# Decode rows of the output projection as fp32 products in four column groups of the array

## What is computed

```python
m = jax.nn.sigmoid(ga) * (o_a @ w_pa) + jax.nn.sigmoid(gb) * (o_b @ w_pb)
x = x + _rmsnorm(m @ w_o, g_mq)
h = _rmsnorm(x, g_fp)
f = (jax.nn.silu(h @ w_g) * (h @ w_u)) @ w_d
x = x + _rmsnorm(f, g_fq)
```

## Time and profile before

| | us |
|---|---|
| median of 3 runs (1453.14 to 1455.04) | 1453.59 |
| the profiled execution, its own time | 1453.83 |
| its span, first to last instruction | 1452.1 |
| PE busy | 1434.0 (99%) |
| PE weight loads busy | 1387.8 |
| DVE busy | 875.2 |
| ACT busy | 627.8 |
| POOL busy | 322.2 |

### The profile page before, as it was taken

How to read it: one execution, slowest core, us unless ns; L and a number is a source line. 1 busy time by engine, 2 the same in 40 slices (tenths; PEclk the granted TensorE clock), 3 DMA queues, 4 the chain that set the end, 5 groups by cost and what they waited for, 6 DMA issues and landing times.

```text
span 1452.1 us, 26576 instructions
## 1 busy us (share of the span) xinstructions
PE 1434.0 (99%) x10633; PEld 1387.8 (96%) x10633; DVE 875.2 (60%) x1539; ACT 627.8 (43%) x1259; POOL 322.2 (22%) x288
## 2 busy tenths in 40 slices
PE   7999999999999999999999999999999999999998
PEld 6999999999999999997789999999999999999997
DVE  7735766313424438483678966777775667667565
ACT  7335555335524532244676433333333335443561
POOL 2022222000000016060002354655362220010111
PEclk9999999999999999999999999999999999999999
DMA  7112323613212126215564334555543349223632
GB/s 233 30 50 77 97 79 112 184 57 108 73 30 77 30 87 205 61 54 176 196 200 140 99 120 153 193 179 204 167 146 118 95 148 377 82 81 108 228 141 102
DMA packets 168381, 184.90 MB, mean 127 GB/s; under 512 B 17514, under 2 KB 128370, under 8 KB 166852
## 3 DMA queue, kind: packets, MB, share of 16 engines
q1 hardware_dynamic: 164368, 171.09, 36.6%
q0 software_dynamic: 2720, 7.89, 1.8%
q10 hardware_dynamic: 1172, 4.23, 0.7%
HBM read 140.73 MB, written 42.45 MB: 126 GB/s over the span
## 4 chain that ended last, share of the span: by engine, by line
PE 93%; DVE 4%; DMA 1%; ACT 1%; issue 1%; DVEq 0%; ACTq 0%
PE bank L1057 7%; PE bank L1059 6%; PE bank L1058 6%; PE psAB L1601 3%; PE bank L1601 3%; PE psAB L1603 3%; PE psAB L1602 3%; PE bank L1602 3%; PE bank L1603 3%; PE psT L1053 3%; PE bankC L1603 2%; PE bankC L1601 2%; PE bankC L1602 2%; PE bank L1158 2%; PE bank L1160 2%; PE bank L1159 2%
## 5 line engine op out<-in xcount | busy, mean ns | idle before, releaser
L1057 PE MATMUL bank<-h_hi,w_hi 128*128 128x344 f32 x464 | 155.8, 336 | 3.0 <-DVE h_lo L2472 3.0
L1059 PE MATMUL bank<-h_hi,w_lo 128*128 128x344 f32 x464 | 149.3, 322 | 0.0
L1058 PE MATMUL bank<-h_lo,w_hi 128*128 128x344 f32 x464 | 149.2, 322 | 0.0
L2229 ACT ACTIVATE s_hi<-raw 128x512 fp32r<-128x512 f32 x126 | 78.7, 627 | 106.7 <-PE psAB L1603 91.3
L1601 PE MATMUL psAB<-f,s_hi 128*128 128x258 f32 x400 | 113.5, 284 | 0.1
L1603 PE MATMUL psAB<-f,s_lo 128*128 128x258 f32 x400 | 112.7, 282 | 0.0
L2459 DVE TENSOR_TENSOR w_lo<-w_raw,w_hi 128x1024 fp32r<-128x1024 f32 x53 | 65.5, 1235 | 61.3 <-ACT w_hi L1764 61.3
L3027 DVE TENSOR_TENSOR s_lo<-raw,s_hi 128x512 fp32r<-128x512 f32 x126 | 94.7, 778 | 2.7 <-ACT s_hi L2229 2.6
L1057 PEld LDWEIGHTS bank<-h_hi,w_hi 128*128 128x128 f32 x464 | 88.3, 190 | 7.3 <-POOL w_lo L3329 3.2
L1601 PE MATMUL bank<-f,s_hi 128*128 128x258 f32 x328 | 93.0, 283 | 0.6 <-DVE ev L3207 0.4
L1603 PE MATMUL bank<-f,s_lo 128*128 128x258 f32 x328 | 92.6, 282 | 0.0
(11 more groups left out here) (686 smaller groups left out, 4937.0 us busy)
## 6 DMA issues: line engine op xcount, KB each, us to landing
raw<-in_w_gate SPq DMA_DIRECT2D x26, 512.0 KB, 4.9
raw<-in_w_up SPq DMA_DIRECT2D x26, 512.0 KB, 6.2
w_raw<-in_w_in SPq DMA_DIRECT2D x24, 512.0 KB, 4.4
w_raw<-in_w_out SPq DMA_DIRECT2D x24, 512.0 KB, 3.7
tp<-in_w_down SPq DMA_DIRECT2D x22, 512.0 KB, 4.6
t_rows<-tp SPq DMA_DIRECT2D x11, 1024.0 KB, 5.1
a_rows<-ab SPq DMA_DIRECT2D x18, 516.0 KB, 2.7
sx_raw<-in_w_in SPq DMA_DIRECT2D x18, 512.0 KB, 5.1
```

The source lines that it names most:

```text
L1057: mm(out[:, 0:TG], w_hi[par][:, ws], hi[:, k, tgc[tg]], start=first, stop=False)
L1058: mm(out[:, 0:TG], w_hi[par][:, ws], lo[:, k, tgc[tg]], start=False, stop=False)
L1059: return mm(out[:, 0:TG], w_lo[par][:, ws], hi[:, k, tgc[tg]], start=False, stop=last)
L2229: fn(slot(q, 0), split_source(q), ACT.Copy).then_inc(sp_hi, 1)
```

## The change

The decode tile is computed without the split. POOL now writes `m_dec` as 32 fp32 columns (four copies of `m_hi + m_lo` of the 8 decode rows). For each of the two channel blocks of a unit, PE makes four fp32 products of 128 weight columns each, with `m_dec` stationary and `w_raw` moving, into PSUM rows 32 c to 32 c + 31, columns 0 to 127. ACT copies the four pieces to their places in the row, and the two sums on DVE are gone. Because PE now reads `w_raw`, SP waits for the decode tile of the unit two before ahead of loads 10 to 17, by new steps of `md_s` (six more of them, one for each unit of group 1 but the last of each half) or by `y_full`. PE takes the decode tile first in units 8 to 10 and 12 to 14. Two of the six turns move up by one token tile or stay behind another one (`F_TURNS`).

```diff
-        m_dec, _ = at("m_dec", [P, KD, 40], F32R, R[3] + 4 * NT * 4)
+        m_dec, _ = at("m_dec", [P, KD, 32], F32, R[3] + 4 * NT * 4)
@@ SP
-                sp.wait_ge(md_s, 1 + 4 * i + 4)
+                sp.wait_ge(md_s, 7 + 4 * i + 4)
...
                     u = U0["wo"] + 8 * g + n
+                    if 10 <= 8 * g + n < 18:
+                        h, q = divmod(8 * g + n - 10, 4)
+                        if q < 3:
+                            sp.wait_ge(md_s, 3 * h + q + 2)
+                        else:
+                            sp.wait_ge(y_full[h], 5)
                     load_w(u, u % 2, chunks(A["w_out"][0], 256 * (n % 4), 2, 512 * (n // 4), 512), 2)
@@ PE
-            F_TURNS = {(1, 5, 1): 0, (1, 6, 1): 1, (1, 7, 1): 2, (2, 3, 0): 3, (2, 4, 0): 4, (2, 7, 0): 5}
+            F_TURNS = {(1, 5, 0): 0, (1, 6, 0): 1, (1, 7, 1): 2, (2, 3, 0): 3, (2, 4, 0): 4, (2, 7, 0): 5}
...
-                    both = psY[h][i][0:40, :]
-                    k, ws = 2 * q, [slice(512 * b, 512 * b + 512) for b in range(2)]
-                    mm(both, m_dec[:, k, :], w_hi[par][:, ws[0]], start=(k == 0), stop=False)
-                    mm(out, m_hi[:, k, tok[t]], w_lo[par][:, ws[0]], start=False, stop=False)
-                    mm(out, m_hi[:, k + 1, tok[t]], w_lo[par][:, ws[1]], start=False, stop=False)
-                    return mm(both, m_dec[:, k + 1, :], w_hi[par][:, ws[1]], start=False, stop=(k + 2 == KD))
+                    for b in range(2):
+                        k = 2 * q + b
+                        for c in range(4):
+                            ins = mm(psY[h][i][32 * c:32 * c + 32, 0:P], m_dec[:, k, :],
+                                     w_raw[par][:, 512 * b + P * c:512 * b + P * c + P], start=(k == 0), stop=(k == KD - 1))
+                    return ins
...
-                    for i in range(3):
+                    for i in ((1, 0, 2) if g == 1 and q < 3 else (0, 1, 2)):
                         if q == 0 and g:
-                            pe.wait_ge(y_free[h], 6 if (g, h, i) == (2, 0, 1) else 3 * g - 2 + i)
+                            pe.wait_ge(y_free[h], 3 * g - 2 + i)
...
+                        elif ORDER[3 * g + i] == 8:
+                            ins.then_inc(md_s, 1)
@@ ACT
-                    fn(T[0:NS, 0:512], bank[i][32:40, :], ACT.Copy).then_inc(y8_low, 1)
+                    for c in range(4):
+                        ins = fn(T[0:NS, P * c:P * c + P], bank[i][32 * c:32 * c + NS, 0:P], ACT.Copy)
+                    ins.then_inc(y_free[0], 1)
...
-                        fn(T[0:NS, 512:D], psY[1][i][32:40, :], ACT.Copy).then_inc(y8_low, 1)
-                        act.wait_ge(y_free[0], 6)
-                        act.wait_ge(y8_sum, 1)
+                        for c in range(4):
+                            ins = fn(T[0:NS, 512 + P * c:512 + P * c + P], psY[1][i][32 * c:32 * c + NS, 0:P], ACT.Copy)
+                        ins.then_inc(y8_row, 1)
+                        act.wait_ge(y8_row, 1)
                         act.wait_ge(f_t, 3)
@@ DVE
-                part_ = tb[1][1][0:NS, 512 * h:512 * h + 512]
-                dve.wait_ge(y8_low, h + 1)
-                v.tensor_tensor(part_, part_, psY[h][1][0:NS, :], ALU.add).then_inc(y8_sum if h else y_free[0], 1)
...
-                if g == 2:
-                    dec_sum(1)
...
-                if g == 1:
-                    dec_sum(0)
@@ POOL
             for r in range(4):
-                g_.tensor_copy(m_dec[:, :, NS * r:NS * r + NS], m_hi[:, :, SEQ:NT])
-            g_.tensor_copy(m_dec[:, :, 32:40], m_lo[:, :, SEQ:NT]).then_inc(md_s, 1)
+                ins = g_.tensor_tensor(m_dec[:, :, NS * r:NS * r + NS], m_hi[:, :, SEQ:NT].bitcast(F32),
+                                       m_lo[:, :, SEQ:NT].bitcast(F32), ALU.add)
+            ins.then_inc(md_s, 1)
```

More of the change, by code:

```diff
@@ L529, in build @@
         far_s = sem("m_far_started")
-        md_s, y8_low, y8_sum = sem("m_dec_then_t_sums_done"), sem("y1_dec_low_copied"), sem("y1_dec_summed")
+        md_s, y8_row = sem("m_dec_used_then_t_sums_done"), sem("y1_dec_copied")
         x1_out = [sem("x1_stored_" + x) for x in ("01", "2", "34", "8", "567")]
@@ L2950, in x1_term @@
                     st.link(ins)
-            def dec_sum(h):
-                part_ = tb[1][1][0:NS, 512 * h:512 * h + 512]
-                dve.wait_ge(y8_low, h + 1)
-                v.tensor_tensor(part_, part_, psY[h][1][0:NS, :], ALU.add).then_inc(y8_sum if h else y_free[0], 1)
             def x1_add(p):
@@ L3451, in t_sums_of @@
             def t_sums_of(i):
-                b, n = tp[i % 2], 1 + 4 * i
+                b, n = tp[i % 2], 7 + 4 * i
                 pool.wait_ge(w_in_s[i % 2], 16 * (UNITS // 2) + 32 * (i // 2 + 1))
```

## The result

The changed kernel takes 1455.32 us, median of 20 runs (1451.74 to 1458.58), where the kernel before took 1453.12 in 20 runs beside it (1452.01 to 1455.04): ratio 1.0016, 95% interval 1.0009 to 1.0022. It is 2.2 us slower. The profiled execution took 1455.19 us against 1453.83 before, 1.36 us more.

A forecast was written before the change was run, and what follows sets the result against it. PE bounds the kernel, busy 1434.0 of 1452.1 us. Plus 0.9 for unit 13, minus 1.5 for units 13 to 17: -0.6, so 1453.2 profiled; median 0.24 lower, forecast 1453.0 us, range 1450.9 to 1456.4.

The forecast's parts named there:

- The decode tile: PE, output projection: a visit takes 0.76 us (0.44 products, 0.32 entering and leaving column groups), 0.17 less than before.
- groups one by one: Rival: PE's column groups don't run side by side; a visit takes 2.08 us, total +8.5, 1462; chance 0.03.
- the instruction stream: Rival: PE's instruction stream bounds the small products; worked from rows +0.6 us on each of eight visits, 1457.1; chance 0.02.
- Units 10 to 12: Output projection (unit: one weight tile, three token tiles): starts stay where DVE puts them, so five decode tiles' gain is lost.
- Load 13: w_raw load for unit 13: issued 2.4 to 2.7 us later, takes 4.0 us, so unit 13 starts 0.9 late.
- Units 13 to 17: Output projection on PE: 21.5 us in place of 22.99, 1.5 less.
- the wait ahead of unit 17: PE's wait there, some 0.8 of the 1.5 us saved, goes because DVE's second decode sum goes.
- load 17: w_raw load for unit 17: just hidden if it takes 3.8 us, 1.6 late if it takes 5.7.
- unit 18: End of the affected stretch on PE: starts at 726.2 in place of 726.81, 0.6 us earlier.
- "Passed on to the end": From unit 18 to the kernel's end: the gain of 0.6 us there carries through to the total.
- The clock: PE idle ahead of unit 13 could bring half clock, 1.7 us more, 1458.1; mainly this made 0.08 of slower outcomes.
- The first rival: Loads 13 and 17 both take 5.7 us: +2.8, 1456.4, or 1458.1 with a clock fall; chance 0.11.

The follow-up runs named there:

- before_late13: Kernel before with one more wait in the load queue: weight load 13 held until unit 11 has ended, old arithmetic kept; 1457.55 us, ratio 1.0027.
- three_buffers: Changed kernel with a third w_raw buffer, so a load waits for the decode tile three units back instead of two; 1452.91 us, ratio 0.9998.
- three_pad128: Changed kernel with a third w_raw buffer and 64 small transposes (128 instructions) added to PE's program; 1451.66 us, ratio 0.9989.
- before_short_sum: Kernel before with DVE's two decode sums over 4 columns of 512, nothing of the change added; 1452.38 us, ratio 0.9994.
- before_plus192: Kernel before, arithmetic untouched, with 96 small transposes (192 instructions) added ahead of PE's real work; 1454.81 us, ratio 1.0012.
- after_pad128: Changed kernel with 64 small transposes (128 instructions) added in PE's first idle stretches; 1454.70 us, ratio 1.0007.
- after_again: The changed kernel measured once more, no edit; 1455.25 us, ratio 1.0017.
- after_pad64: Changed kernel with 64 already satisfied waits put in PE's program, which became 32 instructions more; ratio 1.0019.
- decode_first: Changed kernel with the decode tile first in units 11 and 15 too, SP's and ACT's waits moved with it; 1453.84 us, ratio 1.0009.
- three_pad64: Changed kernel with a third w_raw buffer and 64 already satisfied waits put in PE's program; 1452.15 us, ratio 0.9993.

## Why the prediction failed

**The decode tile: right.** Forecast 0.76 us a visit, measured 0.78 by PE's starts: the bursts of four lie 0.11 us apart, 0.44 us, and entry, exit and dearer first step are 0.34 us where 0.32 was forecast. The two small rivals, groups one by one and the instruction stream, fall with it. The Trainium skill, "TensorE: Matmul & The Clock Gate", "Wait — 56ns, not 53.3ns?", gives its figure of about 62 ns for hardware decode off; by it 16 records would be 1.0 us where they took 0.57 with the exit, so that case is not the one measured here.

**Units 10 to 12: right.** They started at 692.11, 695.89 and 699.68, inside the three ranges given. DVE set them, and the gain of units 8 to 12 was lost.

**Load 13: the term that was mis-sized.** Its issue was forecast for 698.2 and came at 698.20. "I take 4.0 us, near the median" was wrong: it took 5.08, and unit 13 started at 705.73 instead of 704.7. In thirteen of the fourteen profiles this load took 4.3 to 6.4 us (4.0 only in before_late13, where it went out last of all, at 699.7); the row for it in the kernel before said 5.7, and I put that down to the x load ahead of it, which is gone by 698. But in the kernel before a store of x rows (697.03 to 702.64) and load 14 (from 699.41) also lay beside it, and these stay beside it in after: the DMA engines were busy for 0.96 of load 13's time, as before, and for 0.61 to 0.69 of loads 10 to 12's. In before_late13, where it took 4.0, they were busy for 0.72. The other loads of the stretch were the wrong sample: the nearest row for load 13 was load 13. How long it takes from run to run is not explained by this: 4.3 us in three_buffers and 6.4 in three_pad128, issued at 694.8 in both. Units 13 to 17 then took 21.48 us for the 21.5 forecast, the wait ahead of unit 17 went with DVE's sum as said, and load 17 was just hidden (landed 720.41, w_hi from 720.50). So unit 18 was 1.01 us behind its forecast (727.21 for 726.2): 1.03 from load 13, the rest of the sum was right to 0.02. These are times from the first instruction; 0.24 us of them stood at unit 0 already, so that, counted from there, load 13 went out 0.24 us earlier than forecast. The wait ahead of unit 17 was worth less than its term in the sum: 0.5 us in before_short_sum for the "some 0.8".

**"Passed on to the end": the step that failed.** I looked only for what moves with unit 18. From 727 to 812 us nothing much happened, and then 0.9 us came on top, through a chain that I had priced at nothing: 192 more PE instructions, a packet of them at another time, a weight load 1 us longer, GpSimd and VectorE in each other's way, PE 0.9 us idle. The prediction counted the records of the visit as time on PE and never as bytes to be fetched. before_plus192 gives the chain with the old arithmetic (+1.08), after_pad128 and three_pad128 take most of it away again (0.64 and 0.98 us less at that place than after and three_buffers).

**The clock: under-weighted.** The first rival had "an idle PE could bring the same, 1.7 us more" at loads of 5.7 us. It came at loads of 4.8 to 5.4 us already, in three of the four profiles with the changed kernel's loads (after_again, after_pad64, after_pad128, not after), at 1.6 us (6.03 for 4.42).

**The sum as it was.** Forecast for a profiled execution was 1453.2 us, and 1455.19 is 2.0 more: 1.0 at unit 18, 0.9 at 813. Against the kernel before the profiles differ by 1.36 us: 0.24 at the start of the stage, 0.16 in units 0 to 17, 0.9 at 813, the rest small. The medians differ by 2.2. Of the 0.8 left over 0.7 lies with the kernel before: its profiled execution, with a fall at 588, was 0.7 us above the median of its 20 runs, that of after 0.1 below. So the medians differ by something that the two profiles don't show. Falls of the clock, of 1.5 to 1.6 us each, would do it at one more in every second execution, and the executions of after with a mean granted clock of 0.993 or 0.994 were its four slowest (1457.9 to 1458.6). An estimate from the mean granted clocks: 0.9955 over the 31 executions of after and after_again, 0.9962 over the 98 of the kernel before beside the experiments, 0.0007 less or 1.0 us. That this is all of it was not shown, nor that it comes of the wait ahead of unit 13: before_plus192, which had no wait there, has a mean clock of 0.9954 too, and decode_first, which waited 0.6 us, times up to 1457.86. Two kernels with no long wait at unit 13 have such a remainder too: against the kernel before, the profile of before_plus192 is 0.35 us longer (1454.18) and its median 1.5, and that of three_buffers 1.3 us shorter (1452.55) and its median 0.6.

**What the change is worth.** With no load waiting for the decode tile, units 0 to 17 took 2.3, 1.1 and 0.8 us less than before (three_buffers, three_pad64, three_pad128; one profile each). With the packet out of the way too the time is 1.6 us less (three_pad128, ratio 0.9980 to 0.9998); three_pad64, with the packet in place, took 1.2 us less (0.9984 to 1.0002), so the times don't tell what part of it is the packet's.

## What to carry to other kernels

Before you price a load by the median of its neighbours, look whether that very load has been the slow one before, and what it lies beside. A change in the number of PE's instructions moved every later packet of its instruction fetch: where a gain or a loss turns up far from the edit, look in the DMA view for a packet of kind "instruction" in the load that ends last, and try the kernel with some idle instructions at its start. Where VectorE and GpSimd work on the same load within half a microsecond of each other, a load that lands 1 us later can decide which one goes first, and the time with it. Before you split the difference of two medians by two profiles, look how far each profiled execution lies from its own median.

## What the runs showed of the hardware

- One instruction packet of 16 KB holds a DMA engine for 0.96 us (1.1% of sixteen engines over 5.45 us, DMA view of after), and the 512 KB load around it took 5.1 to 5.5 us in seven profiles where it took 4.2 to 4.8 in the seven without. The Trainium skill, "Runtime: NRT & Kernel Launch", Instruction fetch mechanics, gives the size: blocks of 16 KiB, 256 instructions; the page of after agrees with 16 KB each.
- s_lo on DVE stood still while POOL's sum ran: it ended 0.55 us behind POOL's end in after (789.51 and 788.96) and in before_plus192 (788.55 and 788.00), and its own length alone is 0.68. Where s_lo had begun 0.04 us ahead of a sum, as in before, s_lo took its 0.68 and the sum 1.80, for 1.63 in after: the one that began first kept its time, though the sum behind lost only 0.17. The Trainium skill, "SBUF — State Buffer", Who interferes with whom, has the rule: "Issue order, not op shape, decides who blocks." These rows agree as to who is held up.
- Entering and leaving the column groups cost 0.09 to 0.10 us in and about 0.24 out with the dearer first step (0.50 us long for 0.39), 0.34 together in after; four fp32 products in four groups take 0.11 us a step of 128 columns.
- Two waits that follow each other in a program became one instruction, 0.11 us apart on an idle PE; the 96 transposes of 4x4 did not.
